# The first expert's weights loaded and split inside the projection's block, and three changes of order in the projection

## What is computed

```
y = mamba2_mixer(hm, ...)                                  # ends in (y @ w_out)
x = layer_norm(ALPHA * x + (1 + g1) * y, ln_g[0], ln_b[0])
hm = x * (1 + sc2) + sh2
probs = softmax(hm @ w_router + b_router)                  # best group, then top 2 in it
hg, hu = xs @ w_gate[e], xs @ w_up[e]                      # tokens sorted by expert
ye = (silu(hg) * hu) @ w_down[e]
x = layer_norm(ALPHA * x + (1 + g2) * sum_of_two(gate * ye), ln_g[1], ln_b[1])
```

## Time and profile before

| | us |
|---|---|
| median of 3 runs | 2989.3 |
| lowest, highest | 2984.44, 2990.38 |
| the profiled execution | 2990.43 |
| its span | 2988.6 |

### The profile page before, as it was taken

One profiled execution on the slowest core, in us unless ns is written; L12 is line 12 of the kernel. 1 busy time (PEld: TensorE's weight loads), 2 busy tenths in 40 slices (PEclk: granted clock), 3 DMA queues, 4 the chain that ended last, 5 costly groups with the idle time before them and its releaser, 6 DMA issues. The chain is left out here.

```text
span 2988.6 us, 41030 instructions
## 1 busy us (share of the span) xinstructions
PE 2718.9 (91%) x14603; PEld 2316.1 (77%) x14603; DVE 2218.1 (74%) x2647; ACT 1315.9 (44%) x1655; POOL 1489.7 (50%) x755
## 2 busy tenths in 40 slices
PE   3899999999999999999979999949999999999920
PEld 2688888888889888888868888747888888888820
DVE  7678777777878777887863333458888888888857
ACT  4443333343433333343431111126777777777733
POOL 0133433343343334334432222126899999999963
PEclk9899999999999999999989999959999999999965
DMA  8844544444553544455252322249878869678676
GB/s 271 310 183 145 211 155 171 174 171 161 184 211 137 190 175 165 166 184 197 95 169 106 105 105 105 78 152 373 319 269 293 307 242 341 233 259 288 245 273 247
DMA packets 253185, 610.13 MB, mean 204 GB/s; under 512 B 15968, under 2 KB 98560, under 8 KB 244864
## 3 DMA queue, kind: packets, MB, share of 16 engines
q1 hardware_dynamic: 228208, 525.26, 49.2%
q0 software_dynamic: 11520, 41.95, 3.7%
q10 hardware_dynamic: 13328, 41.21, 3.4%
HBM read 600.75 MB, written 99.89 MB: 234 GB/s over the span
## 5 line engine op out<-in xcount | busy, mean ns | idle before, releaser
L1933 DVE TENSOR_TENSOR piece_lo<-piece_raw,piece_hi 128x2048 fp32r<-128x2048 f32 x187 | 563.3, 3031 | 102.5 <-ACT piece_hi L2040 101.3
L2040 ACT CAST piece_hi<-piece_raw 128x2048 fp32r<-128x2048 f32 x280 | 526.7, 1910 | 217.8 <-issue 77.8
L1933 POOL TENSOR_TENSOR piece_lo<-piece_raw,piece_hi 128x2048 fp32r<-128x2048 f32 x93 | 558.9, 6010 | 34.5 <-ACT piece_hi L2040 32.3
L574 PE MATMUL op<-hm,w_hi 128*128 128x512 f32 x2048 | 533.4, 406 | 45.2 <-DVE hm L1236 45.2
L1110 DVE SCALAR_TENSOR_TENSOR cv<-ub,par,cv 128x512 f32<-128x512 f32 x384 | 381.0, 992 | 157.1 <-ACT cv L833 147.9
L574 PEld LDWEIGHTS op<-hm,w_hi 128*128 128x128 f32 x2048 | 379.8, 190 | 119.5 <-DVE hm L1236 45.2
L524 POOL TENSOR_TENSOR xw<-xw,t 128x512 f32<-128x512 f32 x64 | 98.7, 1543 | 488.6 <-DVE t L1178 488.5
L589 PE MATMUL pz<-wz_hi,hm 128*128 128x256 f32 x2048 | 296.9, 290 | 1.1 <-DVE wz_lo L1088 0.5
L589 PEld LDWEIGHTS pz<-wz_hi,hm 128*128 128x128 f32 x2048 | 266.8, 192 | 7.4 <-DVE wz_lo L1088 3.9
L574 PE MATMUL op<-hm,w_lo 128*128 128x512 f32 x1024 | 254.9, 391 | 0.0
L505 POOL TENSOR_TENSOR xdt<-xw,tab 128x512 f32<-128x512 f32 x64 | 70.4, 1100 | 369.3 <-ACT xw L852 345.1
(11 more groups left out here) (338 smaller groups left out, 5698.2 us busy)
## 6 DMA issues: line engine op xcount, KB each, us to landing
hm<-hm_parts SPq DMA_DIRECT2D x30, 4096.0 KB, 13.9
piece_raw<-in_w_gate SPq DMA_DIRECT2D x94, 1024.0 KB
piece_raw<-in_w_up SPq DMA_DIRECT2D x94, 1024.0 KB
piece_raw<-in_w_down SPq DMA_DIRECT2D x92, 1024.0 KB
decay<-acum_rows SPq DMA_DIRECT2D x32, 1024.0 KB
w_raw<-in_w_in SPq DMA_DIRECT2D x48, 512.0 KB, 7.5
expert_out<-ye ACTq DMA_DIRECT2D x46, 512.0 KB
w_ada_part<-in_w_ada_t SPq DMA_DIRECT2D x32, 512.0 KB, 3.9
```

The source lines that it names most:

```text
L574: mm = nc.tensor.matmul(pj[m % 2][:], wp[m][:, kk, :], hm[b][:, hp, kk, :], start=q == 0, stop=q == 3 * KK - 1)
L1933: v.tensor_tensor(lo[q][:], raw[q][:], hi[q][:].bitcast(F32), ALU.subtract).then_inc(lo_done[q], 1)
L2040: nc.scalar.copy(hi[q][:], raw[q][:]).then_inc(hi_done[q], 1)
```

## The change

- The experts' block goes. `experts` now adds its programs to the block of mixer and projection, behind `out_projection`; so the block's end, the clearing block and the start of the next block between them are gone. Only one clearing block is left between experts and output, and `k.used` then holds the semaphores of mixer, projection and experts. The experts' semaphores reuse the numbers of the mixer's, which GpSimd clears inside the projection, behind tile 1 (`of_mixer`, 93 of them).
- The experts' buffers are laid over those of the mixer and the projection (`experts_buffers`, with unused gaps so that each lies over what is free in time).
- SyncE, behind its last step of the projection, waits for the last product (`o_mm`) and loads the six pieces; then the row g2.
- ScalarE casts pieces 0 and 1 between tile 15's store of h2 and its two copies of h2t, pieces 3 and 2 behind the exponential of choose(1), pieces 5 and 4 behind the loop. VectorE makes low parts 0 and 1 in front of choose(1) and 2 behind it. GpSimd makes 3 and 5 behind its loop.
- TensorE's `turn(i-1)` stands behind both products in step 1 too.
- choose(0) moves on VectorE from the end of step 14 to step 15, behind tile(14). ScalarE's exponential for it moves into step 15, behind the store of h2 and the wait for `lg_mm`, in front of the copies of h2t.

The wait in `logits` and everything else in the loops is as before. The diff, cut:

```diff
@@ mixer_steps
-        o = projection_buffers(k, ctx, first)
+        o = projection_buffers(k, later, first)
+        later.close()
+        k.semaphores, kept = own_sems, len(k.used)
...
+        of_mixer = k.used[kept:]
+        k.semaphores = stay
+        out_sems = projection_semaphores(k)
+        own_sems.close()
+        x = experts_buffers(k, ctx)
...
+        experts(nc, k, x, o, block, first, out_sems)
@@ out_projection, sync
         loop(sp, step)
+        sp.wait_ge(o_mm, 2 * TT)
+        for q in range(x.PIECES):
+            sp.dma_start(x.raw[q][:], first_weights(k, q)).then_inc(x.loaded[q], 16)
+        sp.wait_ge(xm_done, TT)
+        sp.dma_start(x.g2[:], k.adad[3].partition_broadcast(P)).then_inc(x.g2_in, 16)
@@ gpsimd
+            if not in_loop(i, 2) and in_loop(i, 1):
+                for s in of_mixer:
+                    pool.sem_clear(s)
 
         loop(pool, step)
+        for q in (3, 5):
+            pool.wait_ge(x.hi_done[q], 1)
+            nc.gpsimd.tensor_tensor(x.lo[q][:], x.raw[q][:], x.hi[q][:].bitcast(F32), ALU.subtract
+                                    ).then_inc(x.lo_done[q], 1)
@@ tensor
-            final = isinstance(i, int) and i == TT - 1
-            if before and not final:
+            behind = isinstance(i, int) and i in (1, TT - 1)
+            if before and not behind:
                 turn(i - 1)
             if here:
                 products(b, 1)
-            if final:
+            if behind:
                 turn(i - 1)
@@ scalar
                 act.dma_start(k.h2d[bass.ds(j * P, P), :], h2[:]).then_inc(h2_out, 16)
+                if isinstance(j, int) and j == TT - 1:
+                    first_high(0)
+                    first_high(1)
                 if in_loop(j, 1, TT):
                     act.wait_ge(lg_mm, j)
+                if isinstance(j, int) and j == TT - 2:
+                    power(0, EARLY)
...
                 if isinstance(j, int) and j == TT - 1:
                     power(1, TT - EARLY)
+                    first_high(3)
+                    first_high(2)
...
             if in_loop(i, 1, TT - 1):
                 split(i + 1, 1 - b)
-            if isinstance(i, int) and i == TT - 2:
-                power(0, EARLY)
...
         loop(act, step, 1)
-        act.wait_ge(xa_out, 16 * TT)
-        act.wait_ge(h2_out, 16 * TT)
+        first_high(5)
+        first_high(4)
@@ vector
             if in_loop(i, 1):
                 tile(i - 1, 1 - b)
+            if isinstance(i, int) and i == TT - 1:
+                choose(0, 0, EARLY)
             if in_loop(i, 1, TT - 1):
                 low(i + 1, 1 - b)
             if not in_loop(i, 1):
                 mix_rows()
-            if isinstance(i, int) and i == TT - 2:
-                choose(0, 0, EARLY)
...
         loop(dve, step, 1)
+        first_low(0)
+        first_low(1)
         choose(1, EARLY, TT - EARLY)
+        first_low(2)
         dve.wait_ge(pos_mm, 2)
@@ program
             stage(nc, k, mixer_steps, first)
-            if stop > 2:
-                stage(nc, k, experts, first)
```

More of the change, by code:

```diff
@@ L196, in mixer_steps, with first_weights @@
+def first_weights(k, q):
+    if q < 4:
+        return k.d["w_gate" if q < 2 else "w_up"][0].rearrange("(kk p) f -> p kk f", p=P)[:, (q % 2) * 4:(q % 2) * 4 + 4, :]
+    return k.d["w_down"][0].rearrange("(kk p) f -> p kk f", p=P)[:, :, (q - 4) * 512:(q - 3) * 512]
 def mixer_steps(nc, k, first):
     with ExitStack() as ctx:
-        own = ExitStack()
+        own, later, own_sems = ExitStack(), ExitStack(), ExitStack()
+        stay = k.semaphores
         sb, ps, sem = k.makers(own)
@@ L1462, in _ @@
             low_y(1, 1)
-        out_projection(nc, k, o, block, first, Tail(
+        out_projection(nc, k, o, x, out_sems, of_mixer, block, first, Tail(
             ymm=(ymm, SUBS * STEPS), yn_tr=(yn_tr, 2 * STEPS), y_done=(y_done, 2 * STEPS), gt=(gt, 2 * STEPS),
@@ L1917, in step @@
-            def step(t, b):
-                load(t + 1, range(GU))
-                if in_loop(t, 1):
-                    load(t, range(GU, PIECES))
-            load(0, range(PIECES))
-            sp.dma_start(g2[:], k.adad[3].partition_broadcast(P)).then_inc(g2_in, 16)
-            sp.wait_ge(x_in[0], 16)
-            loop(sp, step)
-        def low_part(eng, v, q, t):
-            if in_loop(t, 1):
-                eng.wait_ge(used[q], t)
-            eng.wait_ge(hi_done[q], t + 1)
-            v.tensor_tensor(lo[q][:], raw[q][:], hi[q][:].bitcast(F32), ALU.subtract).then_inc(lo_done[q], 1)
@@ new lines, in load, with step, low_part @@
+                    sp.wait_ge(lo_done[q], t)
+                    sp.dma_start(raw[q][:], w, cond=fresh > 0).then_inc(loaded[q], 16)
+                else:
+                    sp.dma_start(raw[q][:], w).then_inc(loaded[q], 16)
+        def step(t, b):
+            load(t + 1, range(GU))
+            if in_loop(t, 1):
+                load(t, range(GU, PIECES))
+        sp.wait_ge(x_in[0], 16)
+        loop(sp, step)
+    def low_part(eng, v, q, t):
+        if in_loop(t, 1):
+            eng.wait_ge(used[q], t)
+        eng.wait_ge(hi_done[q], t + 1)
+        v.tensor_tensor(lo[q][:], raw[q][:], hi[q][:].bitcast(F32), ALU.subtract).then_inc(lo_done[q], 1)
@@ new lines, in _, with fetch, step @@
+    @block.gpsimd
+    def _(pool):
+        def fetch(t, b):
+            if in_loop(t, 2):
+                pool.wait_ge(x_tr, 2 * (t - 1))
+                pool.sem_inc(k.passed, 1)
+            nc.gpsimd.tensor_copy(ix[b][:], k.ids[:, bass.ds(t, 1)]).then_inc(ix_ready, 1)
+            pool.wait_ge(ix_ready, t + 1)
+            pool.sem_inc(k.passed, 1)
+            nc.gpsimd.indirect_dma_start(out=xg[b][:], out_offset=None, in_=k.h2d[:],
+                                         in_offset=bass.IndirectOffsetOnAxis(ap=ix[b][:], axis=0)
+                                         ).then_inc(x_in[b], 16)
+        def step(t, b):
+            fetch(t + 2, b)
+            low_part(pool, nc.gpsimd, 3, t + 1)
+            if in_loop(t, 1):
+                low_part(pool, nc.gpsimd, 5, t)
+        pool.wait_ge(arrived.h2_out, 16 * TT)
+        pool.wait_ge(ids_ready, 1)
+        pool.sem_inc(k.passed, 1)
+        fetch(0, 0)
+        fetch(1, 1)
+        last = loop(pool, step)
+        for b in range(2):
+            pool.wait_ge(x_in[b], 16 * (last + 2))
+            pool.sem_inc(k.passed, 1)
```

626 lines of the change are left out of this document (313 added, 313 removed).

## The result

| us | before | changed |
|---|---|---|
| median of 4 runs each | 2986.95 | 3007.6 |
| lowest, highest | 2984.44, 2990.38 | 3005.59, 3009.55 |
| the profiled execution | 2990.43 | 3008.37 |
| its span | 2988.6 | 3006.3 |

The changed kernel takes 1.0069 times as long, interval 1.0054 to 1.0084. The forecast was 3009.

What follows compares the result with a forecast made beforehand. TensorE, busy 91% of the span, was taken to bound most stretches. The terms, chiefly +13.2, +8.8, +9.1 and -9.98, sum to +19.1 on the profiled 2990.4 us: 3009.5, stated as 3009, range 2999 to 3016.

Steps and rivals of the forecast that it cites:

- Part 1: First turn behind both products: 1.6 us gained, 2.2 charged for TensorE's restart, 93 clears hidden; +0.6 us.
- Part 2, the stall: At logits(13), TensorE waits for p_ready of choose(0), 10.7 us later than before, plus 2.5 restart; +13.2 us.
- The rival without a stall: At logits(13), p_ready is there by 1904.73, so 13.2 us fall away: 2996.3; chance 0.12.
- Part 2, what it gives back: From turn(14) to turn(15), the store of `r` leaves earlier because tile 14's h2 is ready early; -2.5 us.
- it leaves some 2 us behind it, after the two copies: ScalarE's store of `r` leaves some 2 us behind turn(14), after two h2t copies, where it was 4.5.
- Part 3: At tile 15, ScalarE's two casts delay the h2t copies that logits(15) awaits; weight loads cost nothing; +2.85 us.
- first_low(0) and (1) lie under that: Before choose(1), VectorE's low parts 0 and 1 are hidden under the +2.85 us of ScalarE's casts.
- Part 4: In choose(1), VectorE's small instructions wait for GpSimd's low parts 3 and 5; +8.8 us, bounds 0 to 9.0.
- the rival of 3000.7: In choose(1), the small instructions don't wait for GpSimd, so the 8.8 us fall to zero; chance 0.15.
- Part 5: Merged blocks: the 9.98 us gap before routing goes, but clearing 185 semaphores before the output adds 9.1 us.
- Part 6: At the experts' first tiles, earlier loads for tile 1 spare waits; -4.0 us, from 0 to -6.6.
- The rival of a longer stall: TensorE stays at 1.2 GHz for most of products(15), or loads hold up `r`: 3016 to 3020; chance 0.05.

Runs made afterwards that it cites:

- e1: The changed kernel with choose(0) and its exponential back in step 14: 2997.89 us, 1.0031 of the kernel before.
- e2: The changed kernel with logits(13) moved on TensorE between products(15,0) and products(15,1): 2994.05 us, 1.0012 of the kernel before.
- e7: The changed kernel with ScalarE's casts 0 and 1 behind the h2t copies, VectorE's low parts 0 and 1 under the id matmuls: 3004.55 us, ratio 1.0047.
- e5: The kernel before with semaphores cleared by ranges in all three clearing blocks, nothing else: 2976.35 us, 0.9948 of the kernel before.
- e3: The changed kernel with GpSimd's low parts 3 and 5 back behind its first two gathers: 2998.82 us, 1.0029 of the kernel before.
- e8: The changed kernel with logits(13), turn(0), casts, VectorE's three and GpSimd's low parts moved, and clears by range: 2965.85 us, 0.9915 of the kernel before.
- e4: The changed kernel with each clearing block clearing by ranges, the clears behind tile 1 unaltered: 2992.69 us, 1.0010 of the kernel before.
- the second comparison: The changed kernel unaltered, timed again against the kernel before: 3009.16 us, ratio 1.0058.

## Why the prediction was right

*Part 1 (+0.6, measured +0.43, +0.3 in the mean over all kernels).* Right in reason; so small a size isn't told from nothing. The two terms were both a little larger: products(2,0) begin 2.07 us sooner behind turn(0) (1.6 was said), and from there to turn(1) it takes 2.50 us more (2.2 was charged). TensorE's idle spell moved from in front of turn(0) to behind it, and its releaser is the low half of tile 2. The clears of 93 semaphores were hidden, as forecast.

*Part 2, the stall (+13.2, measured +13.65).* The wait grew by 10.5 us (0.83 to 11.34) where 10.7 was said. The restart was the smaller term, and it was mis-sized: 2.5 was charged; logits took 1.65 us more (3.59 for 1.94) and the first eight products 1.5 more (3.63 for 2.12), 3.1 together. The 0.9 us for the third instruction of choose(0) beside GpSimd came out as 1.49 - 0.59 = 0.90. e1 and e2 show that the place of choose(0) in front of a fixed logits(13) is the cause. The rival without a stall is refuted.

*Part 2, what it gives back (-2.5, measured -2.88).* The step "it leaves some 2 us behind it, after the two copies" failed in a small way: the issue stood at 1942.74, in the queue behind the first copy, 1.08 us behind turn(14), while the second copy had yet to run. The gain passed the 2.7 that the prediction had called the most, by 0.2. That bound took rank(0), which stands in front of turn(15), to be as long as before; but in before it had run in part at the low clock:

```profile
1933.61:1945.37 11.76, 11.76 (x55) 8.45 (x55) 3.04 (x6) 1.13 (x1) 1.15 (x2) 0.87 0.25 89
...
1945.23:1955.52 10.29, 10.29 (x56) 7.79 (x55) 4.03 (x7) 1.24 (x1) 0.55 (x1) 1.00 0.84 292
```

The first line (columns as in the earlier trace rows) is rank(0) of before, the second that of the changed kernel: 11.76 us at a mean clock of 0.87, 10.29 at 1.00. The chain through `r` set the gain: its store left 3.4 us earlier behind turn(14), its load went out 3.2 earlier, and h2 of tile 15 came 2.9 earlier. e1 took it away again (17.58).

*Part 3 (+2.85, measured +2.57).* The mechanism was right, the closeness in part luck. e7 shows that casts and low parts cost 3.3 us; turn(15), for which the prediction charged what it took before, gave 0.9 back by running in 1.09 us instead of 1.97. And "first_low(0) and (1) lie under that" held by nothing to spare: VectorE went from the second low part straight into choose(1). The loads of the weights were costed at nothing, 1 to 2 us if they held up `r`. From the issue of tile 15's load of `r` to its first use it took 3.73 us, 3.43 in before; over the eight other kernels in which those loads stand behind it, it took 3.44 to 3.68, and in e5, which has none there, 3.57. So nothing to speak of, as said.

*Part 4 (+8.8, measured +8.50).* The step on which the rival of 3000.7 hung. Bounds of 0 and 9.0, the value taken by the row of 6.66 us, and e3 puts it all on GpSimd. The Trainium skill ("SBUF — State Buffer", Who interferes with whom) says that of two instructions that need the ports which VectorE and GpSimd share, the one that starts second waits for the whole of the first. The trace agrees: VectorE's row at 1969.07, begun 0.13 us after GpSimd's, ends when half of 8.98 us is over, and the next one at 1973.52 ends with the other half. The prediction cited the rule for two SBUF inputs only. The first of the two that waited is a TENSOR_SCALAR with one, and the same section counts tensor_scalar and copy among the instructions that can take the shared ports. The COPY of e8 at 1990.55, 4.40 us long, agrees too, and so does the low part at 1959.36, which stood behind a GpSimd instruction that began 0.05 us earlier.

*Part 5 (-9.98 and +9.1, first_low(2) +1.0).* The gap fell by 9.08 where 8.98 was the sum, and the clears came back as +9.45. The wait for the block is 12.7 us where 12.4 was worked out from 0.067 us for each semaphore. e4 and e5 show the mechanism from both kernels.

*Part 6 (-4.0, measured -2.73).* The mis-sized term. It took the copies of xt to come 3.7 us earlier once the loads go out with the first product; counted from tile 0's tanh they came 2.7 us earlier (8.20 for 10.93). But now all the loads of tile 1 go out within a few us, at 2018.09 and 2019.31, and ScalarE's casts of pieces 1, 2 and 3 (2028.03, 2030.74, 2033.45) start 2.71 us apart, each after a wait of 0.37 to 0.80 us for its DMA. So a piece of 1 MB lands every 2.7 us here, and the last of them, not the time of issue, sets the copies. The own range of 0 to -6.6 held it.

*The sum.* Eight terms off by 0.1 to 1.3 us, with both signs, give 19.9 for 19.1. The median of the changed kernel (3007.6) is 1.4 under the forecast. So close a hit is in part luck: the start up to turn(0), which no edit touches, was 2.2 us shorter in the profiled execution, and the median of before itself moved from 2989.3 to 2986.95 with one more execution. By the medians the step is 20.7 us, and 17.9 in the second comparison. The rival of a longer stall (3016 and more) is refuted by the clock of the changed kernel in the window behind the wait:

```profile
1915.00:1942.00 27.00, 27.00 (x114) 22.31 (x114) 13.20 (x35) 0.55 (x1) 1.37 (x1) 0.89 0.00 1
```

A mean of 0.89 over 27 us is some 5.9 us at 1.2 GHz (0.11 / 0.50 x 27) and the rest at 2.4.

What stays open: whether the restart of 1.7 us in e1 behind a wait of 0.88 us, where before had none behind 0.83 and e5 none behind 1.01, is chance or has a cause, and the like of the clock at tile 1 in e1 and e3; and how often e8's full clock at logits(15) comes about.

## What to carry to other kernels

When an instruction moves on one engine, list every engine that waits for its semaphores and look where those waits stand in their programs: here moving choose(0) was worth 2.9 us, and left in front of an unmoved wait it cost 13.7. Work put on GpSimd "under" a chain of small VectorE instructions with their operands in SBUF was not hidden: of its 8.98 us the chain grew by 8.5. Count such work as if it stood in the chain. Merging two blocks removes a boundary only if the work that stood at it, here the clears, is made cheaper or hidden; issuing that work as ranges brought nearly as much at that boundary (8.3 us for 9.1) without merging anything. With ranges in both (e5 and e8) the merge by itself is worth 1.4 us at the boundary that went, costs 0.6 at the one that is left, and lets the first loads and splits begin early, which is worth 3.0 at tile 1.

## What the runs showed of the hardware

- Clearing semaphores one by one makes the others wait 12.7 us for 185, 9.3 for 137 and 3.3 for 48. Cleared by ranges of numbers the same three waits are 1.1, 1.0 and 0.5 us.
- A VectorE instruction on 128x12 elements waited 4.42 us for one of GpSimd's, and a COPY of 128x16 int32 4.40 us (e8; 4.51 in e3), with a single operand each; a 128x512 product with one operand in PSUM passed in 0.67 us.
- TensorE behind an idle spell of 11 us needs about 3.1 us more for its next sixteen small and eight dense matmuls; with 1.20 us of idle time in front of turn(15) and 0.78 behind it (e7) logits(15) took 3.62 us, with none in front and the same 0.78 behind (e8) 1.97; behind 0.88 us (e1) it lost 1.7 us in one execution, and behind 0.83 us (before) and 1.01 us (e5) nothing.
